# Two modulation products in each norm behind the output projections, FFN gate sums in the MLP's up blocks, and a z block split one step sooner

## The chip, the cores and the metric

The kernel runs on one core of a Trainium2 chip, as one launch. The metric is device time in microseconds (us), the median of the timed executions. All stages run on one core's engines, in program order on each engine: TensorE (PE), VectorE (DVE), ScalarE (ACT), GpSimd (POOL) and the DMA queues of SyncE (SP), ACT and POOL.

## The reference, cut to what matters

A two-layer diffusion step over 640 tokens (512 latent, 128 context), model width 1024, all in float32.

```python
for l in range(2):
    mc, ml = modulation(c_ctx, w_mod, b_mod), modulation(c, w_mod, b_mod)   # silu(c) @ w_mod (1024 x 6144) + b_mod, cut into 6
    dc, dl = mixer(modulate(xc, mc[0], mc[1])), mixer(modulate(xl, ml[0], ml[1]))   # layer 0: attention + SSD, layer 1: pooling
    xc, xl = layer_norm(ALPHA * xc + mc[2] * dc), layer_norm(ALPHA * xl + ml[2] * dl)
    fc, fl = mlp(modulate(xc, mc[3], mc[4])), mlp(modulate(xl, ml[3], ml[4]))       # square(relu(h @ w_up)) @ w_down
    xc, xl = layer_norm(ALPHA * xc + mc[5] * fc), layer_norm(ALPHA * xl + ml[5] * fl)
```

The vectors `m[2]` are the mixer gates and `m[5]` the FFN gates. Each `w_mod` is 24 blocks of 1024 x 256, so there are 48 modulation products in the program; every one of them needs a block of 1 MB loaded from HBM.

## The kernel before, in words

**Weights.** `weight_stream` lists all weight blocks of 1 MB in the order in which SP loads them: ("mod", layer, block), ("in", ...), ("out", ...), ("up", ...), ("down", ...). SP issues them strictly in that order (`load`); each waits until its buffer's last user is done. Blocks of kind "mod" are used as they are (`raw_block`). All others are first split into a high and a low part: ACT writes the high one (`split_hi`, line 1418, tile `whi`), DVE the low one (`split_lo`, line 1912, tile `wlo`), because a projection is done as three matmuls of rounded halves. There are two positions for such halves. `OUT_SLOT` and `ATT_SLOT` say by hand which buffer a block uses late in layer 0 and around the mixer of layer 1.

**Modulation products.** `mod_product(m)` (lines 813 to 825) is 16 small matmuls of one raw block into a PSUM bank. `mod_rows(m)` on ACT copies the result to `modrow` (line 1427), `store_rows(m)` issues two small DMAs from ACT's queue that put it into HBM (line 1433). The first 8 stand in the head; 32 "sites" (m = 8 to 39) are spread over the later mixer: 10 in the SSD stage (the even ones of 20 steps) and 22 in attention; m = 40 and 41 follow the last down projection of layer 0, and m = 42 to 47 follow the first six of the eight products of the pooling mixer. Once a gate's four blocks are stored, POOL loads them as rows (`load_gate_rows`), PE sums them (`gate_sum`, line 839), DVE adds the bias (`gate_bias`, line 1942), PE turns them (`gate_turn`, line 844), ACT copies and stores (`copy_gate`, `store_gate`), and POOL spreads the gate over all partitions (`spread_gate`, a DMA of 1 MB). The FFN gates (numbers 1 and 3) do this inside `project_out`.

**The SSD stage.** Ten steps j = 0 to 9 stand in a loop on each engine. On PE, step j is: `project_in` (24 matmuls), `decays(j)`, `turn_qk`, the site's product if there is one, `chunk_y(j-1)`, `pair_products(j)`. `chunk_y(j-1)` waits for DVE's `weigh_pairs(j-1)` (lines 2142 and 2145, counted in `m_ok`). On ACT, step j is `evac_qk`, `decays(j)` (line 1527), the site's copy or store, and in steps 2 and 8 `split_hi` of the weight blocks 9 and 10. On DVE, step j is `weigh_pairs(j-1)`, `evac_in` of the step's projection (lines 2109 to 2121), in steps 3 and 9 `split_lo` of blocks 9 and 10, and `chunk_sum` in even steps. Block 10 is the first z block; PE's projection after step 9 needs it. ACT and DVE run their instructions in order.

**The norms.** In `project_out` the ten groups of the second half of the columns run in the order `LAST`, with three turns of the normalised tokens between them. After the last group PE goes on with `first_units` of the MLP (line 783), which waits for DVE's low halves of the first three token tiles (`halves`, line 2400, semaphore `ln_lo`). They wait for ACT's `affine` (line 1708).

**The pooling mixer.** PE does eight products (f = 0 to 7, line 774), the first six with a modulation product behind them. Product f waits for ACT's evacuation of product f-2 (`px_f`, line 1859). ACT's step f is that evacuation, the high half (line 1862), a store, a quarter of a weight split (f below 4), and the copy of a modulation product (f below 6).

Of the kernel before, what the change touches and what calls it, by code (L numbers as in the profile page):

```python
# [21 lines left out]
KT = D // P  # L22
NT = 5
# [4 lines left out]
BW = 256  # L28
# [53 lines left out]
def weight_stream():  # L82

    s = []
    for q in range(4):
        s += [("mod", 0, q), ("mod", 0, 4 + q)]
        if q < 2:
            s += [("in", 0, C_XBC + BW * q)]
    s += [("in", 0, C_XBC + BW * j) for j in (2, 3)]
    s += [("in", 0, c) for c in (C_V, C_V + BW, 0, BW, 2 * BW)]  # L90
    mods = [(0, b) for b in list(range(8, 12)) + list(range(12, 20))]
    mods += [(1, b) for b in list(range(0, 8)) + list(range(12, 20))] + [(0, b) for b in range(20, 24)]
    for c, n in ((3 * BW, 2), (C_Z, 3), (C_Z + BW, 2)):
        s += [("mod",) + m for m in mods[:n]] + [("in", 0, c)]
        mods = mods[n:]
    s += [("mod",) + m for m in mods[:19]] + [("out", 0, 1)] + [("mod",) + m for m in mods[19:]]
    for layer in range(2):
        if layer == 1:
            s += [("mod", 1, 8), ("in", 1, 0), ("mod", 1, 9)] + [("in", 1, BW * j) for j in range(1, 4)] + [("pool", 1, 0)]
            s += [("mod", 1, b) for b in (10, 11, 20)] + [("out", 1, 0)] + [("mod", 1, b) for b in (21, 22, 23)]  # L100
        if layer == 0:
            s += [("out", 0, j) for j in (0, 3, 2)]
        else:
            s += [("out", 1, j) for j in range(1, 4)]
        s += [("up", layer, 0), ("up", layer, 1)]
        for c in range(NCHUNK - 1):
            s += [("up", layer, 2 * (c + 1)), ("up", layer, 2 * (c + 1) + 1)]
            s += [("down", layer, 2 * c), ("down", layer, 2 * c + 1)]
        s += [("down", layer, 2 * NCHUNK - 2), ("down", layer, 2 * NCHUNK - 1)]
    return s  # L110


def build(nc, A, O):
# [21 lines left out]
    with ctx:  # L135
# [229 lines left out]
        SITES = 32  # L365
        M_TAIL = 8 + SITES
        THIRD_K = mod_k[22]
        POOL_K = w_k[W_IN1 + 4]
        MIX_K = mod_k[M_TAIL]
        OUT_SLOT = dict(zip(range(MIX_K, MIX_K + 17), (4, 0, 2, 1, 0, 1, 0, 3, 4, 1, 0, 3, 4, 1, 2, 0, 3)))  # L370

        ATT_SLOT = dict(zip(range(THIRD_K, THIRD_K + 22), (2, 0, 1, 3, 4, 2, 0, 1, 3, 4, 2, 0, 1, 3, 4, 2, 0, 3, 4, 1, 0, 1)))

# [7 lines left out]
        def raw_block(k):  # L381
            if k >= FIRST_K and raw_slot(k) == 2:
# [113 lines left out]
        AFTER_SUM, AFTER_TURN = M_MIX + 10 + 12, M_MIX + 10 + 14  # L496
# [11 lines left out]
        def tail_bank(m):  # L508
            if m in (M_TAIL, M_TAIL + 1):
                return 4  # L510
            return 6 if m > M_TAIL and m % 2 else 7

        def tail_lo(m):
            return tail_bank(m) * 512 + BW * (m == M_TAIL + 1)

# [79 lines left out]
        def _(pool):  # L595
# [93 lines left out]
            load_gate_rows(1, 3)  # L689
# [44 lines left out]
            def mlp(layer):  # L734

                spill_x(layer)
                fetch_x_again(layer)
# [3 lines left out]
            spread_gate(1)  # L741
# [13 lines left out]
            load_gate_rows(3, 1)  # L755
# [3 lines left out]
            spread_gate(3)  # L759
# [6 lines left out]
        def _(pe):  # L766
# [40 lines left out]
            def mod_product(m):  # L807

                raw_ready(pe, mod_k[m])
                if m < M_MIX:  # L810
                    lo = 6 * 512
                    if m >= 1:
                        pe.wait_ge(mod_row, m)
                else:
                    lo = tail_lo(m)
                    pe.wait_ge(mod_row, m if m <= M_TAIL else m - 1)
# [166 lines left out]
            def site(j):  # L983
                if j % 2 == 0:
                    site_product()
# [208 lines left out]
            def turn(i, t):  # L1194
# [4 lines left out]
                if t == 1 and i != 1:  # L1199
                    pe.wait_ge(gate_cp, i + 2)  # L1200
# [9 lines left out]
            def project_out(layer):  # L1210
# [5 lines left out]
                for j in range(2):  # L1216
                    w = W_OUT[layer] + j
                    pe.wait_ge(lo_done, OPS[w + 1])
                    for t in range(NT):
# [4 lines left out]
                        if layer == 0 and j == 0:  # L1224
# [5 lines left out]
                            if t == 3:  # L1230
                                pe.wait_ge(mod_row, M_TAIL)
                                pe.wait_ge(gate_cp, 1)
                        if layer == 0 and j == 1:
                            pe.wait_ge(mix_lo, t + 1)
                        if layer == 1 and (j, t) == (0, 2):
                            pe.wait_ge(mod_row, 48)
# [14 lines left out]
                gate_sum(2 * layer + 1, (3, 1)[layer], 2, 96)  # L1251
                for n, (j, t) in enumerate(LAST):
                    if n == 2:
                        gate_turn(2 * layer + 1, 2, 128)
# [7 lines left out]
                    last_turns(2 * layer, n)  # L1262

# [91 lines left out]
            def down(layer, d, i=None):  # L1355
# [5 lines left out]
                for t in range(NT):  # L1361
                    g = 5 * d + t
                    if g >= 4:
# [27 lines left out]
            for f in range(KT):  # L1391
# [9 lines left out]
                if f < 6:  # L1401
# [6 lines left out]
        def _(act):  # L1408
# [11 lines left out]
            def mod_rows(m):  # L1420
                lo = 6 * 512 if m < M_MIX else tail_lo(m)
                act.wait_ge(mod_main, m + (2 if m == M_TAIL else 1))
# [160 lines left out]
            for j in range(2 * NT):  # L1583
                evac_qk(2 * NT + j - 1)
                decays(j)
                if j % 2 == 0:
# [3 lines left out]
                if j in (2, 8):  # L1590
                    split_hi(9 + j // 8)
# [5 lines left out]
            for j in range(2 * NT + 1, 4 * NT):  # L1597
                if j < 4 * NT - 2:
                    tanh_z(4 * NT + j)
                if j % 2 == 0:  # L1600
# [111 lines left out]
            def last_norms(i, w):  # L1712
# [9 lines left out]
                if i == 1:  # L1722
                    mod_rows(M_TAIL)
                    mod_rows(M_TAIL + 1)
# [3 lines left out]
                affine(i, 4)  # L1728

# [43 lines left out]
            def mlp(layer):  # L1773
# [5 lines left out]
                for kind, n, i in mlp_steps(act):  # L1779
                    w = w_ord[S.index((kind, layer, n))]  # L1780
                    if kind == "down":
                        split_hi(w + 1, i, (0, 1, 2) if strassen(w + 1) else None)
# [10 lines left out]
                    if late:  # L1793
                        split_hi(w, i, (3, 4, 5))
                        late = False
                    first_quad(layer, n, i)
# [18 lines left out]
            act.wait_ge(mod_main, M_TAIL)  # L1815
            for j in range(1, 4):
                split_hi(W_OUT[0] + j)
            copy_gate(1, 2, 128)
            store_gate(1)
# [3 lines left out]
            store_rows(M_TAIL)  # L1823
            store_rows(M_TAIL + 1)
# [29 lines left out]
            for f in range(KT):  # L1854
# [10 lines left out]
                if 1 <= f < 7:  # L1865
# [3 lines left out]
                if f < 6:  # L1869
# [6 lines left out]
            copy_gate(3, 2, 128)  # L1876
            store_gate(3)
# [18 lines left out]
        def _(dve):  # L1896
# [31 lines left out]
            def vec_bias(n):  # L1928

                layer, j = VECS[n]  # L1930
                dve.wait_ge(mod_tr, GATE_SUM[1])
# [265 lines left out]
            for j in range(2 * NT):  # L2197
# [3 lines left out]
                if j in (3, 9):  # L2201
                    split_lo(9 + j // 8)
# [353 lines left out]
            def mlp(layer):  # L2556
# [7 lines left out]
                for kind, n, i in mlp_steps(dve):  # L2564
# [5 lines left out]
                    if kind == "up":  # L2570
                        split_lo(w + 1)
                        square_low(layer, 2 * n)
# [53 lines left out]
            def project_out(layer):  # L2626
# [12 lines left out]
                gate_bias(2 * layer + 1, 2, 96)  # L2639
# [107 lines left out]
```

## Time and profile before

| | us |
|---|---|
| median of 3 runs | 1446.86 (1446.84 to 1448.26) |
| the profiled execution: its time | 1448.56 |
| the profiled execution: its span | 1446.7 |
| PE busy in the span | 1400.7 (97%) |
| DVE busy | 1040.7 (72%) |
| ACT busy | 543.1 (38%) |
| granted TensorE clock, mean | 0.993 |

The span runs from the first to the last instruction. Busy time of PE counts pipelined matmuls, so a busy PE is not one at its peak. A row of the windows view holds the stretch, its length, the busy time (and count of instructions) of PE, PE's weight loads, DVE, ACT and POOL, then the granted clock, the DMA share and GB/s. A bracket behind a timeline row is the idle time of the engine before it and what ended it. Stages by time: head to 55, convolution projections to 110, SSD stage to 275, attention to 371, output projection of layer 0 to 433, norm and MLP of layer 0 to 865, layer 1's input projection and pooling mixer to 947, output projection to 1007, norm and MLP of layer 1 to the end.

### The profile page before, as it was taken

What the parts mean: (1) busy time and instruction counts of PE and PEld (TensorE: products, weight loads), DVE (VectorE), ACT (ScalarE), POOL (GpSimd) and SP (SyncE); (2) the same over time, 40 slices, a digit from 0 to 9 for tenths busy, and PEclk for the clock granted to TensorE, in tenths of its full rate; (3) what the DMA queues carried; (4) which work ended last, traced back from release to release, by engine and by line L of the source; (5) the groups of instructions that cost most, each with busy time, mean ns of one, the idle gap of its engine ahead of it and who ended that gap; (6) DMA issues with size and microseconds to landing.
All of it is one profiled execution on the core that took longest, in us unless ns stands there. A gap on an engine that the chain in (4) does not pass through costs nothing.

```text
span 1446.7 us, 22838 instructions
## 1 busy us (share of the span) xinstructions
PE 1400.7 (97%) x8806; PEld 1242.8 (86%) x8806; DVE 1040.7 (72%) x1651; ACT 543.1 (38%) x982; POOL 77.2 (5%) x146
## 2 busy tenths in 40 slices
PE   5999999999999999999999999999999999999996
PEld 3899988766789998998898879887999889889985
DVE  3694566677568976776776796967887677667778
ACT  3333353277445332332232254534533223223322
POOL 1300000010200000000000111001100000000011
PEclk8999999999999999999999999999999999999998
DMA  9701234596814322322221723551332222123141
GB/s 316 230 30 59 88 118 132 191 317 221 285 33 143 117 73 67 110 77 69 87 87 58 261 94 108 181 192 39 133 115 76 71 88 88 59 87 116 58 161 73
DMA packets 132300, 177.47 MB, mean 123 GB/s; under 512 B 4170, under 2 KB 104258, under 8 KB 131698
## 3 DMA queue, kind: packets, MB, share of 16 engines
q1 hardware_dynamic: 123250, 146.46, 31.6%
q0 software_dynamic: 7376, 26.76, 5.4%
q10 hardware_dynamic: 1584, 3.01, 0.6%
q8 instruction: 61, 1.00, 0.3%
q14 instruction: 29, 0.24, 0.1%
HBM read 166.94 MB, written 9.27 MB: 122 GB/s over the span
## 4 chain that ended last, share of the span: by engine, by line
PE 80%; DVE 11%; ACT 5%; issue 2%; DMA 1%; ACTq 0%; POOL 0%; SPq 0%; DVEq 0%
PE ps L792 39%; PE ps L1313 20%; PE ps L774 6%; PE ps L783 4%; PE ps L823 3%; DVE convT L2008 2%; PE ps L1121 2%; DVE wlo L1912 2%; ACT h_full L1708 1%; DVE p_pad L2675 1%; ACT tmp L1708 1%; ACT whi L1418 1%; PE ps L1132 1%; ACT e_att L1628 1%; PE ps L1019 1%
## 5 line engine op out<-in xcount | busy, mean ns | idle before, releaser
L1418 ACT ACTIVATE whi<-raw 128x512 fp32r<-128x512 f32 (+2 forms) x193 | 178.6, 935 | 357.8 <-PE ps L792 293.6
L792 PE MATMUL ps<-whi,hid_hi 128*128 128x512 f32 x640 | 249.6, 390 | 0.0
L792 PE MATMUL ps<-wlo,hid_hi 128*128 128x512 f32 x640 | 249.2, 389 | 0.0
L792 PE MATMUL ps<-whi,hid_lo 128*128 128x512 f32 x640 | 249.0, 389 | 0.0
L1912 DVE TENSOR_TENSOR wlo<-raw,whi 128x512 fp32r<-128x512 f32 (+2 forms) x193 | 205.0, 1071 | 26.0 <-ACT whi L1418 22.5
L2341 DVE TENSOR_TENSOR acc<-acc,ps 128x512 f32<-128x512 f32 x120 | 80.3, 684 | 121.9 <-PE ps L792 121.9
L792 PE MATMUL ps<-whi,h_hi 128*128 128x256 f32 (+1 forms) x480 | 157.4, 328 | 2.2 <-DVE wlo L1912 2.2
L792 PE MATMUL ps<-whi,h_lo 128*128 128x256 f32 (+1 forms) x480 | 152.9, 319 | 0.0
L792 PE MATMUL ps<-wlo,h_hi 128*128 128x256 f32 (+1 forms) x480 | 152.8, 318 | 0.0
L792 PEld LDWEIGHTS ps<-whi,hid_hi 128*128 128x128 f32 x640 | 120.1, 188 | 25.3 <-DVE wlo L1912 0.8
L792 PEld LDWEIGHTS ps<-whi,hid_lo 128*128 128x128 f32 x640 | 120.1, 188 | 25.0
L792 PEld LDWEIGHTS ps<-wlo,hid_hi 128*128 128x128 f32 x640 | 120.1, 188 | 24.4
L1313 PE MATMUL ps<-t_hi,whi 128*128 128x320 f32 x384 | 118.7, 309 | 0.0
L1313 PE MATMUL ps<-t_hi,wlo 128*128 128x320 f32 x384 | 118.7, 309 | 0.0
L1313 PE MATMUL ps<-h_lo,whi 128*128 128x320 f32 x384 | 118.6, 309 | 0.0
L1313 PE MATMUL ps<-h_hi,whi 128*128 128x320 f32 x384 | 118.2, 309 | 0.0
L2481 DVE TENSOR_TENSOR tmp<-tmp,ps 128x320 f32<-128x320 f32 x168 | 79.3, 484 | 37.2 <-PE ps L1313 33.1
L792 PEld LDWEIGHTS ps<-whi,h_hi 128*128 128x128 f32 x480 | 91.2, 190 | 10.2 <-DVE wlo L1912 3.2
L792 PEld LDWEIGHTS ps<-whi,h_lo 128*128 128x128 f32 x480 | 91.3, 190 | 6.5
L792 PEld LDWEIGHTS ps<-wlo,h_hi 128*128 128x128 f32 x480 | 91.4, 190 | 5.9
L1313 PE MATMUL ps<-h_hi,wlo 128*128 128x320 f32 x288 | 89.0, 309 | 0.0
L774 PE MATMUL ps<-h_hi,whi 128*128 128x320 f32 x320 | 74.4, 314 | 0.0
(339 smaller groups left out, 2660.6 us busy)
## 6 DMA issues: line engine op xcount, KB each, us to landing
raw<-in_w_up_l SPq DMA_DIRECT2D x32, 1024.0 KB, 5.7
raw<-in_w_down_l SPq DMA_DIRECT2D x32, 1024.0 KB, 5.0
raw<-in_w_mod_l SPq DMA_DIRECT2D x26, 1024.0 KB, 5.5
raw<-in_w_in_l SPq DMA_DIRECT2D x12, 1024.0 KB, 5.3
raw_split<-in_w_mod_l SPq DMA_DIRECT2D x8, 1024.0 KB, 6.3
raw<-in_w_out_l SPq DMA_DIRECT2D x6, 1024.0 KB, 5.7
x_spill<-x_tok POOLq DMA_DIRECT2D x10, 512.0 KB, 2.9
x_tok<-x_spill POOLq DMA_DIRECT2D x10, 512.0 KB, 6.1
```

Of the source, the lines that this page charges most:

```text
L774: mm = pe.matmul(outs[hf], w_of(still, k), a_of(part, k, hf), start=(k == 0 and part == 0 and still == 0), stop=(k == nk - 1 and still == 1))
L783: mm = pe.matmul(out, w_of(still, k), a_of(part, k, hf), start=(k == 0 and part == 0 and still == 0), stop=(k == nk - 1 and still == 1))
L792: mm = pe.matmul(out, a_of(still, k), w_of(part, k), start=(first and k == 0 and part == 0 and still == 0), stop=(last and k == nk - 1 and ...
L823: mm = pe.matmul(ps[32 * g:32 * g + 32, lo:lo + BW], cpad[:, k, :], raw_block(mod_k[m])[:, k * BW:(k + 1) * BW], start=(k < 4), stop=(k >= 4))
L1121: mm = pe.matmul(bank(2 * n + part, 0, keys.shape[-1]), qT[r:r + DH, 2 * n + hp, t * P:(t + 1) * P], keys, start=True, stop=True)
L1313: mm = pe.matmul(bank(b, 0, HALF), WP[still][:, pos // 4, lo:lo + P], moving(part, k), start=(k == 0 and still == 0 and part == 0), stop=( ...
L1418: act.activation(ring_piece(whi, w, g), piece(w, g), ACT.Copy).then_inc(hi_done, 1)
L1708: ins = act.activation(dst, bank(TURN[i % 2][t][f // 4], (f % 4) * P, (f % 4 + 1) * P), ACT.Identity, bias=modT[:, layer, q, f, c:c + 1], ...
L1912: dve.tensor_tensor(ring_piece(wlo, w, g), piece(w, g), ring_piece(whi, w, g).bitcast(F32), ALU.subtract).then_inc(lo_done, 1)
L2008: ins = dve.scalar_tensor_tensor(dst, src, tap, dst, ALU.mult, ALU.add)
L2341: dve.tensor_tensor(dst, dst, bank(4 + g % 4), ALU.add).then_inc(acc_ok, 1)
L2481: dve.tensor_tensor(dst, a, bank(b, 0, HALF), ALU.add).then_inc(comb, 1)
```

## The change

- The sites become 30: of the SSD stage's ten even steps only eight (`SITE_AT`) keep a product; steps 8 and 12 lose theirs. Products 38 and 39 move to the end of `project_out(0)`, behind the last group and its turns and ahead of `first_units`.
- Products 46 and 47 move from behind products 4 and 5 of the pooling mixer to the end of `project_out(1)`. ACT's copies of such a pair stand in `last_norms` ahead of `normed(i, 3)`, their four store DMAs behind `affine(i, 4)`. The blocks' buffers are new ones (`raw_more`), and their loads stand before ("out", 0, 2) and before ("up", 1, 0), with a wait for the end of the scores (`s_mm`) and of the pooling products (`px_mm`).
- Both FFN gates are summed on PE after the MLP's up block 2 and turned after up block 3; bias, copy and store go with them, and POOL's load and spread move behind the norm's share and behind the spill of x.
- The first z block stands in the stream one product sooner, and is split in step 7 on both ACT and DVE (before: step 8 on ACT, step 9 on DVE).

```diff
-    for c, n in ((3 * BW, 2), (C_Z, 3), (C_Z + BW, 2)):
+    for c, n in ((3 * BW, 2), (C_Z, 2), (C_Z + BW, 1)):
...
-            s += [("out", 0, j) for j in (0, 3, 2)]
+            s += [("out", 0, j) for j in (0, 3)] + [("mod",) + m for m in mods[-2:]] + [("out", 0, 2)]
...
-        SITES = 32
-        M_TAIL = 8 + SITES
+        SITES = 30
+        SITE_AT = (0, 2, 4, 6, 10, 14, 16, 18)
+        M_TAIL = 8 + SITES + 2
+        M_NORM = (M_TAIL - 2, M_TAIL, M_TAIL + 6)
...
+                if k == mod_k[M_NORM[0]]:
+                    sp.wait_ge(s_mm, NA)
+                if k == mod_k[M_NORM[2]]:
+                    sp.wait_ge(px_mm, KT)
...
             def site(j):
-                if j % 2 == 0:
+                if j in SITE_AT:
                     site_product()
...
                 spill_x(layer)
+                spread_gate(2 * layer + 1)
                 fetch_x_again(layer)
...
-                if t == 3 and i == 1:
-                    pe.wait_ge(mod_row, M_TAIL + 2)
+                if t == 3:
+                    pe.wait_ge(mod_row, M_NORM[i] + 2)
...
-                gate_sum(2 * layer + 1, (3, 1)[layer], 2, 96)
                 for n, (j, t) in enumerate(LAST):
-                    if n == 2:
-                        gate_turn(2 * layer + 1, 2, 128)
...
+                pe.wait_ge(out_ev, 2 * NT * layer + NT + 2)
+                for m in (M_NORM[2 * layer], M_NORM[2 * layer] + 1):
+                    mod_product(m)
...
+                    if (kind, n) == ("up", 2):
+                        gate_sum(2 * layer + 1, (3, 1)[layer], 7, 0)
+                    if (kind, n) == ("up", 3):
+                        gate_turn(2 * layer + 1, 7, 128)
...
-                if f < 6:
+                if f < 4:
                     mod_product(M_TAIL + 2 + f)
... ACT, SSD steps
-                if j in (2, 8):
-                    split_hi(9 + j // 8)
+                if j in (2, 7):
+                    split_hi(9 + j // 7)
... ACT, last_norms
-                if i == 1:
-                    mod_rows(M_TAIL)
-                    mod_rows(M_TAIL + 1)
+                mod_rows(M_NORM[i])
+                mod_rows(M_NORM[i] + 1)
                 normed(i, 3)
                 affine(i, 3)
                 normed(i, 4)
                 affine(i, 4)
+                store_rows(M_NORM[i])
+                store_rows(M_NORM[i] + 1)
... DVE, SSD steps
-                if j in (3, 9):
-                    split_lo(9 + j // 8)
+                if j in (3, 7):
+                    split_lo(9 + j // 7)
```

## Rows read from the trace of the kernel before

**Rows 1.** The page's slices: granted TensorE clock in tenths.
```profile
PEclk8999999999999999999999999999999999999998
```
**Rows 2.** Waits of PE: releaser, us in total, times, longest.
```profile
PE ps L783 <- DVE h_lo L2400: 5.1, 6, 1.9
...
PE ps L792 <- DVE wlo L1912: 2.2, 3, 1.2
```
**Rows 3.** Timeline of PE, SSD steps 7 to 10: start, duration, engine, line, operation.
```profile
209.84 0.36 PE L792 MATMUL ps<-whi,h_hi 128*128 128x256 f32 x1
...
215.00 0.36 PE L792 MATMUL ps<-whi,h_hi 128*128 128x256 f32 x1
...
220.22 1.10 PE L1019 MATMUL ps<-xb_tok,seg 128*128 128x64 f32 x8
...
221.35 0.36 PE L792 MATMUL ps<-whi,h_hi 128*128 128x256 f32 x1
...
227.92 0.38 PE L792 MATMUL ps<-whi,h_hi 128*128 128x256 f32 x1 [1.16 <-DVE wlo L1912]
```
**Rows 4.** Timeline of ACT, SSD steps 7 and 8.
```profile
215.19 1.42 ACT L1527 ACTIVATE seg<-ps,ssd_small 128x128 f32<-128x128 f32 x5
...
221.86 1.98 ACT L1418 ACTIVATE whi<-raw 128x2048 fp32r<-128x2048 f32 x1
```
**Rows 5.** Timeline of DVE, SSD steps 8 and 9.
```profile
216.64 0.69 DVE L2142 TENSOR_TENSOR seg<-seg 128x512 f32<-128x512 f32 x1 [2.22 <-ACT seg L1527]
217.37 0.69 DVE L2145 TENSOR_TENSOR seg<-seg,ps 128x512 f32<-128x512 f32 x1
...
225.57 2.29 DVE L1912 TENSOR_TENSOR wlo<-raw,whi 128x2048 fp32r<-128x2048 f32 x1 [0.24 <-DVE tmp L2102]
```
**Rows 6.** Timeline of PE in the head, and the windows view behind it.
```profile
29.12 0.65 PE L823 MATMUL ps<-raw_more,cpad 128*32 128x256 f32 x4 [3.10 <-ACT modrow L1427]
...
33.00:38.00 5.00, 5.00 (x21) 5.00 (x21) 3.89 (x9) 3.25 (x3) 0.00 (x0) 0.52 1.10 349
```
**Rows 7.** Timeline of PE where each projection ends and the norm begins.
```profile
432.62 0.39 PE L792 MATMUL ps<-whi,h_lo 128*128 128x512 f32 x1
434.78 0.38 PE L783 MATMUL ps<-h_hi,whi 128*128 128x320 f32 x1 [1.77 <-DVE h_lo L2400]
...
862.57 0.39 PE L792 MATMUL ps<-whi,hid_lo 128*128 128x512 f32 x1
862.89 1.07 PE L823 MATMUL ps<-raw_gate,cpad 128*32 128x256 f32 x16
863.77 1.05 PE L823 MATMUL ps<-raw_pool,cpad 128*32 128x256 f32 x16
...
1008.79 0.38 PE L783 MATMUL ps<-h_hi,whi 128*128 128x320 f32 x1 [1.86 <-DVE h_lo L2400]
```
**Rows 8.** Timeline of ACT in the pooling mixer, steps 4 and 5.
```profile
941.69 0.79 ACT L1859 ACTIVATE tmp<-ps,vecT 128x640 f32<-128x640 f32 x1
...
943.62 0.38 ACT L1427 ACTIVATE modrow<-ps 128x256 f32<-128x256 f32 x1 [0.38 <-issue]
```
**Rows 9.** Timeline of PE: pooling products 6 and 7, then the output projection.
```profile
943.59 0.56 PE L774 MATMUL ps<-hid_hi,whi 128*128 128x320 f32 x2
...
947.21 0.39 PE L792 MATMUL ps<-whi,h_hi 128*128 128x512 f32 x1
```
**Rows 10.** Timeline of PE in layer 1's output projection, around a sum and a turn.
```profile
957.89 0.39 PE L792 MATMUL ps<-whi,h_lo 128*128 128x512 f32 x1
...
958.53 0.50 PE L792 MATMUL ps<-whi,h_hi 128*128 128x512 f32 x1
...
982.15 0.50 PE L792 MATMUL ps<-whi,h_hi 128*128 128x512 f32 x1 [0.74 <-DVE wlo L1912]
```
**Rows 11.** DMA issues: KB each, median us to landing.
```profile
raw<-in_w_mod_l SPq DMA_DIRECT2D x26, 1024.0 KB, 5.5
...
gate<-gate_sums POOLq DMA_DIRECT2D x4, 1024.0 KB, 6.7
```

More of the change, by code:

```diff
@@ L92, in weight_stream @@
     mods += [(1, b) for b in list(range(0, 8)) + list(range(12, 20))] + [(0, b) for b in range(20, 24)]
-    for c, n in ((3 * BW, 2), (C_Z, 3), (C_Z + BW, 2)):
+    for c, n in ((3 * BW, 2), (C_Z, 2), (C_Z + BW, 1)):
         s += [("mod",) + m for m in mods[:n]] + [("in", 0, c)]
         mods = mods[n:]
-    s += [("mod",) + m for m in mods[:19]] + [("out", 0, 1)] + [("mod",) + m for m in mods[19:]]
+    s += [("mod",) + m for m in mods[:19]] + [("out", 0, 1)] + [("mod",) + m for m in mods[19:-2]]
     for layer in range(2):
@@ L99, in weight_stream @@
             s += [("mod", 1, 8), ("in", 1, 0), ("mod", 1, 9)] + [("in", 1, BW * j) for j in range(1, 4)] + [("pool", 1, 0)]
-            s += [("mod", 1, b) for b in (10, 11, 20)] + [("out", 1, 0)] + [("mod", 1, b) for b in (21, 22, 23)]
+            s += [("mod", 1, b) for b in (10, 11, 20)] + [("out", 1, 0), ("mod", 1, 21)]
         if layer == 0:
-            s += [("out", 0, j) for j in (0, 3, 2)]
+            s += [("out", 0, j) for j in (0, 3)] + [("mod",) + m for m in mods[-2:]] + [("out", 0, 2)]
         else:
-            s += [("out", 1, j) for j in range(1, 4)]
+            s += [("out", 1, j) for j in range(1, 4)] + [("mod", 1, b) for b in (22, 23)]
         s += [("up", layer, 0), ("up", layer, 1)]
@@ L363, in mlp_steps @@
                 yield kind, n, None
-        SITES = 32
-        M_TAIL = 8 + SITES
-        THIRD_K = mod_k[22]
+        SITES = 30
+        SITE_AT = (0, 2, 4, 6, 10, 14, 16, 18)
+        M_TAIL = 8 + SITES + 2
+        M_NORM = (M_TAIL - 2, M_TAIL, M_TAIL + 6)
+        THIRD_K = mod_k[20]
         POOL_K = w_k[W_IN1 + 4]
         MIX_K = mod_k[M_TAIL]
-        OUT_SLOT = dict(zip(range(MIX_K, MIX_K + 17), (4, 0, 2, 1, 0, 1, 0, 3, 4, 1, 0, 3, 4, 1, 2, 0, 3)))
-        ATT_SLOT = dict(zip(range(THIRD_K, THIRD_K + 22), (2, 0, 1, 3, 4, 2, 0, 1, 3, 4, 2, 0, 1, 3, 4, 2, 0, 3, 4, 1, 0, 1)))
+        OUT_SLOT = dict(zip(range(MIX_K, MIX_K + 17), (4, 0, 2, 1, 0, 1, 0, 3, 4, 1, 0, 3, 2, 0, 3, 5, 6)))
+        ATT_SLOT = dict(zip(range(THIRD_K, THIRD_K + 24), (2, 0, 1, 3, 4, 2, 0, 1, 3, 4, 2, 0, 1, 3, 4, 2, 0, 3, 4, 1, 0, 5, 6, 1)))
         def raw_slot(k):
@@ L381, in raw_block @@
         def raw_block(k):
+            if k >= FIRST_K and raw_slot(k) > 4:
+                return raw_more[:, raw_slot(k) - 5, :]
             if k >= FIRST_K and raw_slot(k) == 2:
@@ L495, in build @@
         GATE_SUM, GATE_TURN = (9, 14, 16, 18), (10, 15, 17, 19)
-        AFTER_SUM, AFTER_TURN = M_MIX + 10 + 12, M_MIX + 10 + 14
+        AFTER_SUM, AFTER_TURN = M_MIX + len(SITE_AT) + 12, M_MIX + len(SITE_AT) + 14
         ROWS_OF_GATE = (M_MIX + 4, M_TAIL, M_TAIL + 4, M_TAIL + 8)
@@ L508, in tail_bank @@
         def tail_bank(m):
-            if m in (M_TAIL, M_TAIL + 1):
-                return 4
+            for n, first in enumerate(M_NORM):
+                if m in (first, first + 1):
+                    return (5, 4, 5)[n]
             return 6 if m > M_TAIL and m % 2 else 7
         def tail_lo(m):
-            return tail_bank(m) * 512 + BW * (m == M_TAIL + 1)
+            return tail_bank(m) * 512 + BW * (m - 1 in M_NORM)
         def stored_at(m):
@@ L740, in _ @@
             norm_share(0)
-            spread_gate(1)
+            load_gate_rows(1, 3)
             mlp(0)
@@ L758, in _ @@
             norm_share(2)
-            spread_gate(3)
+            load_gate_rows(3, 1)
             mlp(1)
@@ L815, in mod_product @@
                     lo = tail_lo(m)
-                    pe.wait_ge(mod_row, m if m <= M_TAIL else m - 1)
+                    pe.wait_ge(mod_row, m if m < M_TAIL - 1 else m - 1)
                     if m == AFTER_SUM:
@@ L1230, in project_out @@
                             if t == 3:
-                                pe.wait_ge(mod_row, M_TAIL)
+                                pe.wait_ge(mod_row, M_NORM[0])
                                 pe.wait_ge(gate_cp, 1)
@@ L1362, in down @@
                     g = 5 * d + t
+                    if g == 3:
+                        pe.wait_ge(gate_cp, 2 * layer + 2)
                     if g >= 4:
@@ L1421, in mod_rows @@
                 lo = 6 * 512 if m < M_MIX else tail_lo(m)
-                act.wait_ge(mod_main, m + (2 if m == M_TAIL else 1))
+                act.wait_ge(mod_main, m + (2 if m in M_NORM else 1))
                 if m >= M_MIX + 3:
@@ L1585, in _ @@
                 decays(j)
-                if j % 2 == 0:
+                if j in SITE_AT:
                     site_rows()
@@ L1599, in _ @@
                     tanh_z(4 * NT + j)
-                if j % 2 == 0:
+                if j in SITE_AT:
                     site_rows()
@@ L1781, in mlp @@
                     if kind == "down":
+                        if n == 0:
+                            copy_gate(2 * layer + 1, 7, 128)
+                            store_gate(2 * layer + 1)
                         split_hi(w + 1, i, (0, 1, 2) if strassen(w + 1) else None)
@@ L1795, in mlp @@
                         late = False
+                    if n == SU:
+                        act.wait_ge(gate_out, 16 * (2 * layer + 2))
                     first_quad(layer, n, i)
@@ L1864, in _ @@
                     pool_high(KT - 1)
-                if 1 <= f < 7:
+                if 1 <= f < 5:
                     store_rows(M_TAIL + 1 + f)
@@ L1868, in _ @@
                     split_hi(W_OUT[1], None, (f,))
-                if f < 6:
+                if f < 4:
                     mod_rows(M_TAIL + 2 + f)
@@ L1930, in vec_bias @@
                 layer, j = VECS[n]
-                dve.wait_ge(mod_tr, GATE_SUM[1])
+                dve.wait_ge(mod_tr, GATE_SUM[1] - 1)
                 biases = bmodT[:, 48 * layer + 8 * j:48 * layer + 8 * j + 16].rearrange("p (j f) -> p j f", j=2)
@@ L2571, in mlp @@
                         split_lo(w + 1)
+                        if n == 3:
+                            gate_bias(2 * layer + 1, 7, 0)
                         square_low(layer, 2 * n)
@@ L2638, in project_out @@
                         vec_bias(n)
-                gate_bias(2 * layer + 1, 2, 96)
                 if layer == 0:
```

14 lines of the change are left out of this document (2 added, 12 removed).

## The prediction

> **What bounds the kernel now.** I read the page first, then PE's waits, then the timelines of all engines around each edit. PE is at work nearly everywhere, at the full granted clock but for the head and the end [rows 1]. Its waits for other engines are short and few: the longest item is the low half of h at the norms, 5.1 us in six places, and the low halves of weights stop it for 2.2 us in three [rows 2]. So most of the kernel is as long as PE's queue, and an instruction taken from PE is worth its start-to-start time, unless the next one then waits for something else. Each edit turns on that second half of the sentence.
>
> **1. SSD stage: two products gone, the z split one step sooner.** An odd step without product takes PE 215.00 - 209.84 = 5.16 us, the even step after it, with one, 221.35 - 215.00 = 6.35; a product costs 1.19 [rows 3]. Two of them: -2.38. Step 9 lasts 227.92 - 221.35 = 6.57 where 5.16 would do, because the z block's low half is late: a stall of 1.41 that the sooner split takes away. Together that is -3.79, if nothing else gets late.
> But in step 7 both engines now split in the same step. ACT is in `decays(7)` until 215.19 + 1.42 = 216.6 [rows 4] and can only then write the high half, 1.98 us, to 218.6. DVE has finished `evac_in` of step 7 at about 214.4 and now stands at `split_lo`, which waits for that high half: it starts at 218.6 and ends at 220.9 (2.29). Behind it in DVE's queue is `weigh_pairs(7)`, before at 216.64, two operations with starts 0.73 apart and the last one 0.69 long [rows 5]: now done at about 222.3. PE's `chunk_y(7)` waits for exactly that. With its product it started at 220.22; without, it could at 219.1. It will start at about 222.3, a new stall of 3.2. In the kernel before, DVE's split stands a step behind ACT's, and its high half had been there when DVE came. After that the engines catch up: DVE's `weigh_pairs(8)` ends near 226.5 and PE asks for it at 227.5. Step 12's missing product is free of such a wait, since the state updates of DVE there wait for PE, not the other way round. Term: -2.38 - 1.41 + 3.2 = -0.6. Bounds: -3.8 (no new stall) and 0 (the catching up costs another 0.6).
>
> **2. The norms take two products each.** Before, PE starts its last matmul at 432.62 and the first one of `first_units` at 434.78: 2.16 us, of which it is idle 1.77; in layer 1 it is idle 1.86 at 1008.79, so 0.09 more. How long two products take in such a place stands in the trace behind the down projection of layer 0: last matmul 862.57, products at 862.89 and 863.77, the second 1.05 long [rows 7]. The switch to the first matmul of `first_units` overlaps the tail of the second, so it could follow at about 864.8, 2.2 us after 862.57. That is just the hole: cost 0.0 to 0.1 in layer 0, none in layer 1. The hole itself is ended by ACT's and DVE's work on tokens, which the products do not touch. ACT's two copies (0.38 each, the size of [rows 8]) stand ahead of `normed(0, 3)`, where ACT idles 4.2 us for POOL; its four store issues, half a microsecond each, delay the first of the eight `first_relu` by up to 2.0, and DVE is busy with the low half of the fifth tile until 2.1 after that point, so four units later both have caught up. Term: +0.05. Bounds 0 and +0.8 (a wait for ACT's rows or a later start in both norms). If the cover went, the two products would cost their 2 x 1.19 in each norm.
>
> **3. Pooling mixer: products 4 and 5 lose theirs.** A naive count gives -2.38. But ACT paces PE here: the evacuation of step 4 starts at 941.69 and takes 0.79, and ACT's step 5 opens with the modulation copy at 943.62, after high half and store issue [rows 8]. ACT keeps its store of product 45 and loses only the copies (0.28 start to start) and the later stores. Walking on: product 6 waits for the evacuation of step 4, ending at 942.5, where before it started at 943.59 [rows 9]; the evacuation of step 5 runs 943.62 to 944.4, product 7 starts there; a product is 1.76 long, so the output projection starts at 946.25, where it was 947.21. Term: -0.95. Bounds: -2.4 and -0.5.
>
> **4. FFN gates' sum and turn.** In `project_out(1)` the sum costs PE 958.53 - 957.89 less a plain step of 0.23, so 0.4 [rows 10]; the turn is one matmul of 0.27 whose start-to-start share I take as 0.1 (between 0 and 0.3). In the up blocks they cost the same: +0.5 per layer. In layer 0 their old place gives back 0.45: DVE's split of the next weights, which PE needs then, is done some 0.3 before. In layer 1 it gives back nothing, because PE stands idle 0.74 at 982.15 for the low half of the fourth output block; that comes from DVE, which came late from waiting for the mixer's gate. Only the `gate_bias` leaves that DVE chain: -0.1. The idle time grows by what PE saves. Term: +0.05 in layer 0, +0.4 in layer 1. Bounds 0 and +1.0 in sum.
>
> **5. Loads.** The blocks of 38 and 39 are asked for at about 367, with the last two output blocks already under way; 5.5 us each [rows 11], they would be in by 385, and their products run at 433. Those of 46 and 47 are asked for at 946 and go ahead of ("up", 1, 0), which is first split at 1002. Both are free. The gates' spread of 1 MB moves into the MLP, where each weight block is loaded some 10 us ahead. Bounds 0 and +2.6 (the third rival).
>
> **Sum**, against the profiled execution (span 1446.7, time 1448.56): -0.6 + 0.05 - 0.95 + 0.45 = -1.05. So its time would be 1447.5. The profiled execution lies 1.7 above the median; on the median, 1446.86 - 1.05 = 1445.8.
>
> **Rivals.**
> *No collision in step 7.* For it: the place looks free on ACT, which idles 2.7 us ahead of each `evac_qk`, and the z stall is real [rows 2, 3]. Against: ACT's idle time lies ahead of `decays`, not behind it, and both engines are strictly in order. Then -3.8 replaces -0.6: 1442.6.
> *The clock falls* (the slower side). The new stall leaves PE idle from 219.3 to 222.3, 3.0 us. In the head PE idles 3.10 ahead of the matmul at 29.12, and in the window from 33 to 38 the granted clock is 0.52, the 1.2 GHz level instead of 2.4 [rows 6]. Had PE the lower clock from 29.1 to 38, some 9 us, half of these are lost: +4.4, giving 1450.2. Against it: the head's PE was not fully busy before that gap, as it is here, and the idle 1.8 us at both norms [rows 7] left the clock at full [rows 1]. It decides from the point where step 7's wait is as long as the one in the head.
> The Trainium skill ("TensorE: Matmul & The Clock Gate", section "What's actually happening") says that the clock is given by recent activity and falls back to half after an idle window; by that rule a longer stall costs more than its length, and the trace agrees in the head [rows 6], while none of its gaps follows a busy stretch as this one does.
> *The mixer gate of layer 1 arrives late.* Its spread of 1 MB (6.7) is issued near 965; two more blocks (5.5 each) are now in the queues, so that ("up", 1, 0) may land as late as 968 [rows 11]. If the spread then waits out the 2.6 that remain, DVE and after it PE are late by that much: 1448.4. Against: three blocks took 12 us there before, and five at that pace end at 962.6.
> *The moves do nothing at all* (every saving lands in another wait): 1446.9.
>
> **Chances.** Forecast 0.6 (1445.0 to 1446.8); no collision 0.14; clock 0.08; late gate 0.07; nothing 0.11. A measurement of this kernel tells 0.2% (2.9 us) from no change. Faster by more: the first rival and a small tail of the forecast, 0.17; slower by more, above 1449.75: the clock, 0.08; within: 0.75. Range 1442.6 to 1448.6.
>
> **What would show it.** SSD steps: DVE's split in step 7 with an idle time of about 4 ahead of it, ended by `whi`; PE idle some 3 ahead of the `chunk_y` at 222, ended by `seg`; no wait for `wlo` at 227.9; granted clock 1.00 throughout. Norms: two products right behind the last group, and the idle time ahead of line 783 near 0. Pooling mixer: products 5 to 7 start when ACT's evacuations end. Layer 1's fourth output block: a wait for `wlo` of 1.2 or more. Wrong would be: no idle time on DVE in step 7 (then 1442.6), or a norm longer from its last group to the first unit than 2.3 us.

## The result, and the profile after

| | us, median | lowest to highest | runs |
|---|---|---|---|
| before | 1447.28 | 1446.32 to 1448.98 | 9 |
| after | 1451.17 | 1449.62 to 1451.95 | 9 |

The ratio is 1.0023, 95% interval 1.0015 to 1.0032. The change makes the kernel slower, by 3.9 us between the medians and by 2.2 to 4.6 by the interval, where 1.1 us less was forecast, and the time lies above the range. The profiled execution of after has a span of 1449.5 us and took 1451.49; before's are 1446.7 and 1448.56.

The slices of the page show the same row of clock digits as before [rows 1], and nothing in the busy shares tells where 3 us went. PE's waits do (engine, tile, line, releaser; us in total, times, longest):

```profile
PE ps L1027 <- DVE seg L2157: 2.8, 1, 2.8
...
PE ps L1175 <- DVE h_lo L2326: 2.2, 1, 2.2
...
PE ps L791 <- DVE h_lo L2412: 1.4, 4, 0.8
```

The waits at the norms have gone from 5.1 us in six places to 1.4 in four, and those for `wlo` from 2.2 to 0.3 [rows 2]. Two long waits are new, the first two of the list; a third new one, 0.9 us in two places, is that of the pooling products for ACT. To weigh them, I laid the start times of PE's instructions that both kernels have beside each other. The lag of after behind before changes in few places:

| place (time in before) | after minus before there | step |
|---|---|---|
| up to 218, SSD step 7 | -0.1 | |
| 227.92, SSD step 10 begins | +3.3 | +3.4 |
| 245, SSD over | +2.2 | -1.1 |
| 378.88, turn of the last SSD output | +4.3 | +2.1 |
| 402.64, output projection of layer 0 | +3.9 | -0.4 |
| 434.78, behind the norm | +3.9 | 0.0 |
| up blocks of layer 0 | +4.55 | +0.7 |
| 947.21, pooling mixer over | +3.7 | -0.9 |
| 982.15, output projection of layer 1 | +2.2 | -1.5 |
| 1008.79, behind the norm | +2.1 | 0.0 |
| end | +2.8 | +0.6 |

**The SSD steps.** Timelines of PE, DVE and ACT in after (start, duration, engine, line, operation, then idle time and releaser):

```profile
218.82 0.38 PE L945 MATMUL ps<-head,tmp 128*128 128x128 f32 x2
222.03 1.97 PE L1027 MATMUL ps<-xb_tok,seg 128*128 128x64 f32 x8 [2.82 <-DVE seg L2157]
...
224.55 0.41 PE L800 MATMUL ps<-wlo,h_hi 128*128 128x256 f32 x1
224.76 0.41 PE L800 MATMUL ps<-whi,h_lo 128*128 128x256 f32 x1
...
228.58 0.28 PE L800 MATMUL ps<-whi,h_lo 128*128 128x256 f32 x1
228.69 0.28 PE L800 MATMUL ps<-whi,h_hi 128*128 128x256 f32 x1
...
231.25 0.36 PE L800 MATMUL ps<-whi,h_hi 128*128 128x256 f32 x1
```

```profile
218.36 2.29 DVE L1924 TENSOR_TENSOR wlo<-raw,whi 128x2048 fp32r<-128x2048 f32 x1 [4.03 <-ACT whi L1430]
220.57 0.68 DVE L2154 TENSOR_TENSOR seg<-seg 128x512 f32<-128x512 f32 x1
221.29 0.69 DVE L2157 TENSOR_TENSOR seg<-seg,ps 128x512 f32<-128x512 f32 x1
```

```profile
216.36 1.97 ACT L1430 ACTIVATE whi<-raw 128x2048 fp32r<-128x2048 f32 x1
```

ACT's high half, DVE standing 4.03 us for it, the low half ahead of `weigh_pairs`, PE's `chunk_y` at 222.03: the jam is there as drawn. What follows it is not. The eight matmuls at 222.03 take 1.97 us where they took 1.10 [rows 3], and those of step 9 start 0.21 apart until 228.4 and 0.12 apart from 228.58. The windows view (busy time and instructions of PE, PEld, DVE, ACT, POOL, granted clock, DMA share, GB/s):

```profile
215.00:221.00 6.00, 4.21 (x32) 3.73 (x30) 2.64 (x2) 5.09 (x14) 0.00 (x0) 1.00 0.00 1
222.00:228.00 6.00, 5.97 (x28) 5.97 (x29) 3.94 (x10) 0.00 (x0) 0.00 (x0) 0.50 0.53 171
229.00:235.00 6.00, 6.00 (x56) 5.43 (x59) 2.20 (x5) 2.82 (x11) 1.61 (x3) 1.00 0.24 87
```

The granted clock is 0.50, the 1.2 GHz level, where PE resumes behind the 2.82 us of idle time, and 1.00 on both sides. From `chunk_y` to step 10 PE takes 231.25 - 222.03 = 9.22 us; with the same work at the full clock it takes 6.29 (experiment 4: from 221.66 to 227.95). So 2.9 of the +3.4 are the clock, and +0.5 is what the forecast had as +0.6 up to there (3.2 - 1.41 - 1.19). The mean granted clock was 0.991 in eight of after's nine runs; in the ninth it was 0.993, and that is the fastest, 1449.62. It lies 1.5 us below the median and not 2.9, so the clock may have fallen there too, for a shorter time.

**The tail of the SSD outputs.** Timelines of POOL, DVE and PE in after:

```profile
371.59 1.02 POOL L617 TENSOR_TENSOR smisc<-smisc 128x4 f32<-128x4 f32 x1
375.94 1.68 POOL L696 DMA_DIRECT2D sum_rows<-vec_parts  x3 [3.33 <-DMA gate_parts<-modrow]
377.61 2.09 POOL L664 DMA_DIRECT2D x_tok<-in_x_sample  x4
379.73 0.21 POOL L614 TENSOR_SCALAR smisc<-smisc 128x4 f32<-128x4 f32 x1
380.02 1.03 POOL L617 TENSOR_TENSOR smisc<-smisc 128x4 f32<-128x4 f32 x1
```

```profile
381.08 0.16 DVE L2269 TENSOR_TENSOR smisc<-smisc 128x4 f32<-128x4 f32 x1 [5.58 <-POOL smisc L617]
...
382.34 1.88 DVE L2326 TENSOR_TENSOR h_lo<-ps,h_hi 128x512 fp32r<-128x512 f32 x3
```

```profile
383.17 0.63 PE L1175 MATMUL ps<-head,o_tok 128*128 128x128 f32 x4 [2.23 <-DVE h_lo L2326]
```

And POOL at this place in before:

```profile
369.48 1.02 POOL L608 TENSOR_TENSOR smisc<-smisc 128x4 f32<-128x4 f32 x1
370.47 1.68 POOL L687 DMA_DIRECT2D sum_rows<-vec_parts  x3
372.14 2.10 POOL L655 DMA_DIRECT2D x_tok<-in_x_sample  x4
375.45 0.19 POOL L605 TENSOR_SCALAR smisc<-smisc 128x4 f32<-128x4 f32 x1 [1.21 <-ACT osq L1648]
```

The last store of a vector row on ACT's queue, in before and then in after:

```profile
362.62 0.51 ACTq L1433 DMA_DIRECT2D vec_parts<-modrow  x1
```

```profile
370.51 0.49 ACTq L1445 DMA_DIRECT2D vec_parts<-modrow  x1
```

POOL's reading of the vector rows (line 696) waits until this store has landed; the bracket names `gate_parts`, the next store in the same queue. With two products fewer in the SSD stage, the last vector row is produced two places later among the sites of the attention, and its store is issued 7.9 us later, of which 2.1 are PE's lag. By the trace's semaphore records it landed 5.8 us after its issue in before, at 368.45, and 4.9 us after it in after, at 375.39: the two new block loads beside it did not slow it. In before the rows were there when POOL came. In after POOL stands 3.33 us, and behind the wait in its queue is the small reciprocal root of the last token tile, which DVE, then `turn_o` on PE, need: 379.73 instead of 375.45 + 2.2. PE stops for 2.2 us.

**The norms.** PE at the norm of layer 1: last matmul, both products (32 matmuls), first unit of the MLP, 2.23 us from first to last start as forecast, no idle time.

```profile
1008.70 0.39 PE L800 MATMUL ps<-whi,h_lo 128*128 128x512 f32 x1
1009.01 1.93 PE L831 MATMUL ps<-raw_more,cpad 128*32 128x256 f32 x32
1010.93 0.38 PE L791 MATMUL ps<-h_hi,whi 128*128 128x320 f32 x1
```

**Pooling mixer and output projection of layer 1.** Pooling products wait for ACT's evacuation, twice, 0.18 and 0.74. PE there, then POOL and DVE behind it in after, and the same POOL and DVE rows in before:

```profile
947.12 0.53 PE L782 MATMUL ps<-hid_hi,whi 128*128 128x320 f32 x2 [0.74 <-ACT tmp L1873]
...
950.90 0.39 PE L800 MATMUL ps<-whi,h_hi 128*128 128x512 f32 x1
```

```profile
970.31 0.55 POOL L675 DMA_DIRECT2D gate<-gate_sums  x1 [25.21 <-DMA gate_sums<-gate_row]
...
975.34 0.69 DVE L2339 TENSOR_TENSOR gated<-ps,gate 128x512 f32<-128x512 f32 x1 [1.07 <-DMA gate<-gate_sums]
```

```profile
966.35 0.56 POOL L666 DMA_DIRECT2D gate<-gate_sums  x1 [12.37 <-DMA gate_sums<-gate_row]
...
973.08 0.69 DVE L2327 TENSOR_TENSOR gated<-ps,gate 128x512 f32<-128x512 f32 x1 [2.48 <-DMA gate<-gate_sums]
```

The spread of the mixer's gate takes 975.34 - 970.31 = 5.0 us where it took 973.08 - 966.35 = 6.7. DVE gets on 1.7 sooner, and PE's wait of 0.74 for the fourth block [rows 10] is gone.

### The profile page after: what moved, and what is told of

Read it like the earlier page. It is cut to its first block, busy times and chain, and to the rows that moved or that the text cites. A ratio compares the mean times of both kernels' runs of the same rounds, so it can differ in the third digit from the quotient of the medians.

```text
span 1449.5 us, 22838 instructions
## 1 busy us (share of the span) xinstructions
PE 1402.6 (97%) x8806; PEld 1245.2 (86%) x8806; DVE 1040.2 (72%) x1651; ACT 542.9 (37%) x982; POOL 77.2 (5%) x146
## 4 chain that ended last, share of the span: by engine, by line
PE 82%; DVE 10%; ACT 4%; issue 2%; DMA 1%; POOL 0%; ACTq 0%; SPq 0%; DVEq 0%
PE ps L800 41%; PE ps L1319 20%; PE ps L782 6%; PE ps L791 4%; PE ps L831 3%; DVE convT L2020 2%; PE ps L1129 2%; DVE wlo L1924 1%; DVE p_pad L2688 1%; ACT tmp L1720 1%; PE ps L1140 1%; PE ps L1212 1%; ACT e_att L1640 1%; ACT whi L1430 1%; PE ps L1027 1%
```

## Experiments

Two explanations stood at first. **A**: the two stalls (SSD step 7, POOL's wait) and the clock behind the first make up the loss. Its rival **B**: the loss comes from the moved loads and gates, or the clock falls for another reason. The kernel before, run beside them, has a median of 1447.95 (28 runs) for the first four experiments and 1448.29 (28 runs) for the last four, and each ratio is against that. The chip's mean clock of a run also holds the low stretches in the head and at the end, which differ from run to run, so it counts falls in the middle only roughly.

**1. ACT's high half one step sooner.** After, with the collision taken away:

```
-                if j in (2, 7):
-                    split_hi(9 + j // 7)
+                if j in (2, 6):
+                    split_hi(9 + j // 6)
```

> The changed kernel with ACT's high half of the z block in step 6, DVE's low half still in step 7. Theory A (the split collision in step 7 idles PE 2.8 us and this idle time makes the clock fall for 6.8 us): DVE does not wait for whi in step 7, PE runs from step 7 to 10 without a gap, the granted clock stays at 1.00, and step 10's projection starts near 225.2 instead of 231.25; 6.0 us less, 1445.2. Rival B (the fall of the clock has another cause than this gap): the gap goes but the clock falls all the same, 1448.

Measured: 1446.50 (1445.23 to 1448.10, 11 runs), ratio 0.9989, 0.998 to 0.9998. DVE now finds the high half when it comes, and `chunk_y` waits for nothing (timelines of DVE and PE):

```profile
213.88 2.29 DVE L1924 TENSOR_TENSOR wlo<-raw,whi 128x2048 fp32r<-128x2048 f32 x1 [0.24 <-DVE tmp L2133]
```

```profile
218.35 0.89 PE L1027 MATMUL ps<-xb_tok,seg 128*128 128x64 f32 x7
```

Profiled executions differ from before's in the head by up to 1 us either way, ahead of any edit; this one leaves it 0.8 ahead of before. At step 10 it is 3.4 ahead, so 2.6 by the edit, which is 1.2 + 1.4, the product and the z stall; after is 3.4 behind there. The collision with its clock is worth 6.0 us in the trace. The time fell by less than that, since the gap at POOL's wait is still there, and in this execution the clock fell behind that one (timeline of PE, windows view):

```profile
376.74 0.63 PE L1175 MATMUL ps<-head,o_tok 128*128 128x128 f32 x4 [2.57 <-DVE h_lo L2326]
```

```profile
377.50:380.50 3.00, 3.00 (x9) 2.35 (x8) 0.98 (x2) 0.50 (x1) 0.00 (x0) 0.50 1.05 413
381.00:384.00 3.00, 3.00 (x17) 2.48 (x16) 0.69 (x1) 1.82 (x2) 0.00 (x0) 1.00 0.99 394
```

That cost 1.6. In after the gap of 2.23 at the same place had left the clock at 1.00. Seven of the eleven runs have a mean of 0.993 and four have 0.992, so it need not fall here in every run.

**2. POOL's reading of the vector rows behind its last root.** After, with one line moved in POOL's order:

```
-                if t == 3:
+                if t == LAT:
                     pool.wait_ge(mod_tr, GATE_SUM[0])
                     rows_stored(pool, ROWS_OF_VECS)
```

> The changed kernel with POOL's wait for the vector rows and their three loads behind the last rsqrt of the attention, not ahead of it. Theory P (POOL stands 3.3 us at the rows' store, which two fewer sites made later, and the rsqrt behind it holds normed_o of the last tile, DVE's low halves and PE's turn at 383): PE's 2.2 us of idle time at 383 goes, 1449.1. Rival D (the two new block loads of the norm crowd the DMA engines there and make whatever is loaded or stored late): the gap stays, 1451.

Measured: 1449.09 (1447.30 to 1450.44, 11 runs), ratio 1.0006, 0.9997 to 1.0015. POOL:

```profile
375.20 0.19 POOL L614 TENSOR_SCALAR smisc<-smisc 128x4 f32<-128x4 f32 x1 [2.69 <-ACT osq L1660]
375.48 1.03 POOL L617 TENSOR_TENSOR smisc<-smisc 128x4 f32<-128x4 f32 x1
376.48 1.69 POOL L696 DMA_DIRECT2D sum_rows<-vec_parts  x3
```

PE's wait for `h_lo` of line 2326 is gone from the list and there is no jump at 383. Nothing later wanted the vector rows sooner. The stall of 2.8 in step 7 is unchanged, but in this execution the clock fell only after PE had been at work again for 1.5 us, and came back sooner (1.00 in the window from 227 to 230; windows view):

```profile
221.30:222.80 1.50, 1.50 (x13) 1.50 (x14) 1.22 (x7) 0.00 (x0) 0.00 (x0) 1.00 0.82 259
223.00:226.00 3.00, 3.00 (x16) 3.00 (x16) 2.42 (x4) 0.00 (x0) 0.00 (x0) 0.50 0.53 184
```

That cost 1.5 instead of 2.9 (from `chunk_y` to step 10, 221.23 to 228.99, 7.76 us for 6.29). The runs spread over 3 us, in part for this reason: the four under 1448 have mean clocks of 0.992 to 0.994, the seven above 0.990 to 0.992. The clock in the head has a part in it too: from 35.3 to 37.5 it is 1.00 in this execution and 0.50 in before.

**3. Both.**

> Both edits at once. If A and P hold and add up: 1451.2 - 6.0 - 2.1 = 1443.1, which is 4.2 us below the kernel before, faster than both kernels. If one of the gaps only moves: 1445 to 1449.

Measured: 1443.00 (1442.50 to 1444.65, 6 runs), ratio 0.9968, 0.9956 to 0.998: 8 us less than after and 4.6 less than before by the ratios (5.0 by the medians), the clock at 1.00 from the head to the end. Its start times against before: -0.8 in the head, -3.4 at step 10, -4.5 behind the SSD stage, -5.1 in the output projection of layer 0, -4.4 behind that layer's gates, -5.7 in the output projection of layer 1, -6.8 behind its fourth block, -6.2 at the end. A is right in place and size.

**4. The z split alone.** Before, with the split one step sooner but the product of step 8 kept:

```
-                if j in (2, 8):
-                    split_hi(9 + j // 8)
+                if j in (2, 7):
+                    split_hi(9 + j // 7)
...
-                if j in (3, 9):
-                    split_lo(9 + j // 8)
+                if j in (3, 7):
+                    split_lo(9 + j // 7)
```

> The kernel before with the z split alone moved to step 7 on ACT and DVE; step 8 keeps its product. Theory A: DVE waits for whi as in the changed kernel, chunk_y of step 8 starts near 222.1 instead of 220.2, the z stall of 1.4 goes; PE's idle time is about 1.7 us, shorter by the product, and if the length of the gap decides, the clock stays at 1.00: 1447.8. Rival B (the order of work in step 7, not the gap's length, brings the clock down): the clock falls here too, 1450.5.

Measured: 1448.93 (1447.43 to 1452.53, 11 runs), ratio 1.0012, 1.0003 to 1.0021. By itself the split loses: `chunk_y` starts 1.4 behind before though this execution came out of the head 0.5 ahead, so 1.9 late, and the 1.4 of step 9 come back; +0.5 is left. PE:

```profile
221.66 1.10 PE L1019 MATMUL ps<-xb_tok,seg 128*128 128x64 f32 x8 [1.83 <-DVE seg L2145]
...
227.95 0.36 PE L792 MATMUL ps<-whi,h_hi 128*128 128x256 f32 x1
```

The clock stayed at 1.00 here. Three of the eleven runs had a mean of 0.991, and they are the three slowest (1450.6, 1452.0, 1452.5): in this kernel the clock falls sometimes, somewhere in the program. That widens the spread but is not the loss of the median run, 1448.93, whose mean is 0.993; it lies 1.0 above before's median, and the +0.5 of the trace is about half of that. The rest was not followed up.

This execution also shows the gate's spread of layer 1, with the loads in their old order, landing in 5.0 us, and PE without the wait of 0.74, which puts it 1.1 ahead of before behind the fourth block (POOL and DVE):

```profile
966.26 0.56 POOL L666 DMA_DIRECT2D gate<-gate_sums  x1 [12.40 <-DMA gate_sums<-gate_row]
...
971.27 0.69 DVE L2327 TENSOR_TENSOR gated<-ps,gate 128x512 f32<-128x512 f32 x1 [0.77 <-DMA gate<-gate_sums]
```

**5. The gates alone.** Before, with the FFN gates' sums and turns in the up blocks:

```
-                gate_sum(2 * layer + 1, (3, 1)[layer], 2, 96)
...
+                    if (kind, n) == ("up", 2):
+                        gate_sum(2 * layer + 1, (3, 1)[layer], 7, 0)
+                    if (kind, n) == ("up", 3):
+                        gate_turn(2 * layer + 1, 7, 128)
```

> The kernel before with only the FFN gates' sums and turns (and their loads, copies and spreads) moved to the MLP's up blocks. By the prediction: layer 0's output projection gives back 0.45 and its MLP takes 0.5 to 0.7; layer 1's output projection gives back nothing, since PE waits there for wlo either way, and its MLP takes 0.5 to 0.7; +0.7 in all, 1448.6 where the kernel before reads 1447.95. Rival: the sums in layer 1 were on the path there, and the move is neutral: 1447.95.

Measured: 1450.12 (1448.13 to 1452.43, 11 runs), ratio 1.0013, 1.0004 to 1.0022: +1.8, more than expected. In the trace, beside +0.6 in the head: +0.2 in layer 0; in layer 1 the sum and the turn give 0.5, and 0.7 is lost at the fourth block, where PE now waits 1.6 instead of 0.74, so nothing is given back (the spread takes 6.7 here too); the up blocks take 0.6; and the clock falls behind the unfilled hole at the norm (PE's timeline, windows view), which costs about 1.5:

```profile
1009.78 0.38 PE L782 MATMUL ps<-h_hi,whi 128*128 128x320 f32 x1 [1.85 <-DVE h_lo L2401]
```

```profile
1011.00:1014.00 3.00, 3.00 (x13) 3.00 (x12) 2.90 (x7) 0.00 (x0) 1.06 (x2) 0.50 0.38 135
1015.00:1018.00 3.00, 3.00 (x23) 3.00 (x22) 2.93 (x6) 0.43 (x1) 0.00 (x0) 1.00 0.17 35
```

The hole is as long as in before [rows 7], where the profiled execution kept its clock; seven of the eleven runs have a mean of 0.992 here. Before itself is not safe from it: of its 28 runs beside these, seven have 0.991 or 0.992, all at 1449.1 or more. Whether and why it falls more often with the gates moved is not shown; the longer wait 27 us ahead of the hole is a guess.

**6. The mixer's products put back.** Experiment 3, with products 46 and 47, their loads and stores in the pooling mixer again and the norm of layer 1 empty:

```
-                if f < 4:
-                    mod_product(M_TAIL + 2 + f)
+                if f < 6:
+                    mod_product(M_TAIL + 2 + f)
```

> e3_both with products 46 and 47, their loads and stores back behind products 4 and 5 of the pooling mixer, so that layer 1's norm has none. ACT paces the mixer: giving the two products back costs PE 1.0, not 2.4, and the norm's hole of layer 1 is no shorter without them: 1444.0 against 1443.0. Rival (the two products were worth their full length): 1445.4.

Measured: 1445.60 (1444.87 to 1447.83, 11 runs), ratio 0.9985, 0.9976 to 0.9994: 2.6 above experiment 3 by the medians. In the traces, 3.1 apart at the end, 1.2 is there by 366, ahead of this edit; the mixer gives 0.8, and 1.0 more comes at the fourth output block, where PE waits 0.81 for the low half again and the gate's spread takes 5.9 us instead of 4.9. So the moved products bring 0.8 in the mixer, near the 1.0 expected; whether the other 1.0 is theirs hangs on the gate's transfer (below).

**7. The next z block's low half sooner.** Experiment 3, with DVE's `split_lo(11)` in step 13, behind `state_step`:

> e3_both with DVE's low half of the second z block (weights 11) behind the state step of step 13, not behind the evacuation of step 14. PE's wait of 0.3 to 0.7 for this wlo goes: 1442.5. Rival: the split then holds the evacuation of step 14 by 1.0 and w_state after it, and PE waits there instead: 1443.0 or more.

Measured: 1442.87 (1441.67 to 1443.33, 6 runs), ratio 0.9967, 0.9955 to 0.998. No difference from experiment 3 that can be told. In the trace the wait of 0.28 for this `wlo` is gone and PE gains 0.5 there, but as much is lost again near 366, where it now waits 0.43 for a modulation block's load; one execution does not tell whether the edit brought that wait.

**8. A product in the gap.** After, with the product of step 10 in step 8, where PE waits:

```
-        SITE_AT = (0, 2, 4, 6, 10, 14, 16, 18)
+        SITE_AT = (0, 2, 4, 6, 8, 14, 16, 18)
```

> The changed kernel with its product of step 10 in step 8 instead (POOL's wait as in the changed kernel). The collision in step 7 stays, but the product fills 1.2 us of PE's gap: that alone gives 1450.0. If the length of the gap decides on the clock, as e4_z_only has it, the clock stays up in most runs: 1447.5. Rival (any gap of this place brings it down): 1450.0.

Measured: 1449.19 (1447.77 to 1451.82, 11 runs), ratio 1.0008, 0.9999 to 1.0017. PE:

```profile
220.22 1.07 PE L831 MATMUL ps<-raw,cpad 128*32 128x256 f32 x16
223.12 1.10 PE L1027 MATMUL ps<-xb_tok,seg 128*128 128x64 f32 x8 [1.83 <-DVE seg L2157]
```

The idle time is 1.83 instead of 2.82 and the `chunk_y` takes 1.10, and in this execution the clock stayed at 1.00; ten of eleven runs have 0.993 or 0.994, where after had 0.991 in eight of nine. Taking off the head, in which it is 1.0 behind, PE is 3.3 ahead of after behind the SSD stage, with as many products: 2.9 of clock and what the product takes out of the wait, less 0.8 at a longer wait for `w_state`. By the ratios the time is 2.2 better than after's. That is above the 1447.5 expected, and where the rest went was not followed up. POOL's gap is still in it, and the clock held behind it (1.00 from 381.2 to 387):

```profile
381.08 0.63 PE L1175 MATMUL ps<-head,o_tok 128*128 128x128 f32 x4 [2.39 <-DVE h_lo L2326]
```

## Why the prediction was wrong

- **SSD steps.** Right but for the clock: `chunk_y` at 222.03 (forecast 222.3), +0.5 at step 10 without the clock (+0.6), -0.6 for the stage (-0.6).
- **The clock**, +2.9, is the first step of the prediction that failed: the forecast had it at 1.00 throughout and its price at nothing, and left its fall to a rival with a chance of 0.08. That rival named place, cause and sign, and priced the fall at 4.4 us, where the profiled execution lost 2.9. The weighing failed: the gap of the head (3.10) was taken as the measure and the holes of 1.8 as proof of safety. But the stall of 2.82 came with a mean clock of 0.991 in eight runs of nine and brought the clock down in both profiled executions that had it (after and experiment 2); 2.57 and 1.85 did so in experiments 1 and 5, and 2.23 and 2.39 did not in after and experiment 8. So no single length decides here. Experiment 8 suggests that a longer gap makes a fall likelier. The objection that PE was busy around it was no protection, and the remark that no gap of the trace follows a busy stretch overlooks the holes at the norms [rows 7]. The Trainium skill ("TensorE: Matmul & The Clock Gate", section "What's actually happening") describes the chip's watch as free-running, so that the point of transition varies; it says so of the start of a kernel. The traces agree as far as they go: behind the same stall the clock was at 0.50 by 222.0, where PE resumed, in after, and in experiment 2 still at 1.00 for 1.5 us of PE's work.
- **POOL's queue**, +2.1, is the second step that failed, a term put at nothing without a reason: part 1 counted for the two removed products only what they take from PE. The rows that they had produced come later, their reader on POOL waits for the last of them, and what is queued behind this reader was never asked. POOL's queue was not read at all. Without this wait the time would have been 1449.1, as experiment 2 shows, still above the range, which ends at 1448.6; without the fall of the clock it would have been about 1451.2 - 2.9 = 1448.3, just inside it.
- **Norms.** Right: both holes take both products, at 2.2 us from the last matmul to the first unit, +0.0 in each.
- **Pooling mixer.** Right: -0.9 for a forecast of -0.95; the evacuations pace it. (The prediction's 944.4 + 1.76 is 946.2 and not 946.25, which changes nothing.)
- **Gates.** Layer 0: -0.4 and +0.7 for -0.45 and +0.5. Layer 1 in the MLP: +0.6 for +0.5. Alone they give nothing back in layer 1, as forecast (experiment 5). In the whole change the projection came out at -1.5 where -0.1 was forecast: 0.5 for the sum and the turn, which the wait did not take back, and 1.0 where the wait of 0.74 stood, which went with the gate's faster spread. That is luck and not the forecast's doing: the transfer was as fast in experiment 4, where neither gates nor loads are moved.
- **Loads.** The third rival had the right transfer and the wrong sign. It had two more blocks delaying the spread; it lands sooner. In the six profiled executions with the moved products it took 4.9 to 5.2 us, in the four without 6.7, 5.0 (experiment 4), 6.7 and 5.9. So it can be short in either order and was never long with the moves. Why stays open: SP's request for the second up block comes 4.0 to 4.3 us behind the spread's issue in all ten (4.3 in before, 6.7, and in experiment 4, 5.0), so its place is not what differs, and the transfer was not tried by itself.

In sum: the forecast's own terms came out at -2.2 for -1.05, the clock added 2.9 and POOL 2.1: +2.8 in the profiled executions' spans. The medians are 3.9 apart; before's profiled execution lies 1.3 above its median, after's 0.3. Both losses can be had back by one line each, and the rest of the change is then worth 4.6 us (experiment 3); in its profiled execution 1.0 of that came with the gate's short spread.

## What to carry to other kernels

When a step is taken out or put later, follow what it produced: find who reads it, on which queue the reader waits, and what small operation stands behind that wait. When an edit leaves the matrix engine idle in one piece (here 1.85 us was enough once, and 2.39 was not another time), put a chance and a price on the clock, 1.5 to 2.9 us here, and treat the profiled execution as one draw of several. Split a block's high half on one engine a full step ahead of the low half on the other: when the two meet in the same step, everything behind the second one's wait is late by what the first still had to do (here DVE stood 4.03 us).

## What had not been expected of the hardware

- The granted clock fell behind idle times of 1.85, 2.57 and 2.82 us with PE busy on both sides, and held behind 1.83, 2.23 and 2.39. The price of one fall was 1.5 to 2.9 us.
- The fall need not come in the gap. In experiment 2 PE had been at work again for 1.5 us when the clock went from 1.00 to 0.50.
- Whether it falls differs from run to run of one program. Experiment 4 has runs from 1447.4 to 1452.5 and the three with a mean clock of 0.991 are the slowest. Experiments 3 and 7, without a stall of this sort, spread less (1442.5 to 1444.65 and 1441.67 to 1443.33), though over six runs each.
- A transfer of 1 MB (the gate's spread of layer 1's mixer) took 4.9 to 6.7 us in ten executions, with the next block load asked for 4.0 to 4.3 us behind its issue each time.
